# The norm weights travel with x's first tile, and ACT's first transfer is the first key piece

## The chip, the cores and the metric

The kernel runs on one core of one Trainium2 chip. The metric is the device time of one execution in microseconds (us), lower is better. Before the change it is 1268.42 us, the median of three runs (1268.10 to 1268.46).

## The reference, cut to what matters

The reference is a trunk of two layers on x of 512 positions by 1024 features, in float32. Each layer is a token mixer (attention in the first, retention in the second) and a gated MLP. Every one of these four parts begins with an RMS norm that has a weight vector of its own, two vectors for each layer:

```python
def rmsnorm(x, g):
    xf = x.astype(jnp.float32)
    y = xf * lax.rsqrt(jnp.mean(xf * xf, axis=-1, keepdims=True) + EPS)
    return (y * g.astype(jnp.float32)).astype(x.dtype)

for i in range(DEPTH):
    h = rmsnorm(x, norm1_g[i])
    x = x + (attention or retention)(h, ...)
    h = rmsnorm(x, norm2_g[i])
    x = x + conv_ffn(h, ...)
```

What the change touches is the very first step: h = x times norm1_g[0], and the product of h with the key and value columns (256 of them) of attn_w_qkv. The root of the mean square is applied later, to the products.

## The kernel before, in words

x lies transposed in eight tiles of 128 features by 512 positions. Each fp32 operand of a large product is split into two fp32r parts: ACT writes the high part (h_hi, w_hi), DVE the rest (h_lo, w_lo), and `mm3` makes three matmuls of each product (L1293 to L1295). The kernel is one program for each engine, written out in order by hand, with semaphores between them. PE is almost never idle after the first microseconds.

The stage in question is the start. TensorE waits for a zeroed buffer (DVE memset, L677) and then makes WARM_MMS products of zeros, 256 columns wide (L1331); each fp32 product shows in the trace as two passes. It then runs the key and value products: for each of eight feature tiles k, twelve matmuls with 256 columns (four position tiles by three), as soon as w_lo of key piece k (L683) and h_lo of tile k (L662) are there. After these come the query products with 512 columns, in the same way, and so on to the end.

Who brings what in: SP's queue issues, in this order, x tile 0, x tile 1, key piece 2, x tile 2, key piece 3 and so on (L279, L263), and then the first query weights (L282, L283). ACT's queue issues the gain vectors (L337), key piece 0 and key piece 1 (L263), because KV_ACT is 2. An x tile has rows of 2048 bytes, a key piece rows of 1024 bytes, and the gains rows of 128 bytes, always over 128 partitions.

ACT's own order at the start is: its three issues, a small activation that brings its table in (L371), the wait for the gains, then h_hi of tile 0 (L348), w_hi of key piece 0 (L380), w_hi of key piece 1, h_hi of tile 1, and so on. DVE's order is h_lo of tile 0 (L662), w_lo of key piece 0 (L683), w_lo of piece 1, h_lo of tile 1, and so on. Both engines read the gain vectors as a column scalar (`gain[:, norm, m:m + 1]`) in every norm of the kernel, and ACT's wait covers DVE too, since DVE waits for h_hi.

Of the kernel before, what the change touches and what calls it, by code (L numbers as in the profile page):

```python
# [29 lines left out]
P = 128  # L30
D = 1024
S = 512
KT = D // P
# [18 lines left out]
KVC = 256  # L52
KV_ACT = 2
WARM_COLS = 256
WARM_MMS = 6


PAIR_KV = 0
# [21 lines left out]
ROW_F0, ROW_R, ROW_HEAD, ROW_F1 = 0, 1, 2, 1 + R_HEADS  # L80


def trunk(nc, xT, w_kv, w_q, w_ao, w_up0, w_dn0, w_ret, w_up1, w_dn1, gains, conv, gain_col, gain_rot, sinks,
          ident_d, rot_a, rot_r, decay, root_mem, out):
    ctx = ExitStack()
    with ctx:
        def sb(name, shape, dt=F32, scope=ctx):
            return scope.enter_context(nc.sbuf_tensor(name, shape, dt))

        def sem(name):  # L90
            return ctx.enter_context(nc.semaphore(name))


        x = sb("x", [P, KT, S])
        h_hi = sb("h_hi", [P, KT, S], F32R)
        h_lo = sb("h_lo", [P, KT, S], F32R)
        raw = sb("raw", [P, 2, UW])
        w_hi = sb("w_hi", [P, 2, UW], F32R)
        w_lo = sb("w_lo", [P, 2, UW], F32R)
        gain = sb("gain", [P, 4, KT])  # L100
        cvec = sb("cvec", [P, 2, FT, 8])
        ident = sb("ident", [P, P])
        ones = sb("ones", [P, 1])
# [77 lines left out]


        x_in = [sem(f"x_in{k}") for k in range(KT)]
        g_in = sem("g_in")
        c_in = sem("c_in")
        r_in = sem("r_in")
        o_out = sem("o_out")
# [68 lines left out]
        def kv_cols(k):  # L256
            return 1, slice(k * KVC, (k + 1) * KVC)

        def kv_load(eng, k):
            if k < KT:  # L260
                s, cols = kv_cols(k)
                landed = w_loaded[1] if k == KT - 1 else kv_in[k]
                eng.dma_start(raw[:, s, cols], w_kv[:, cols]).then_inc(landed, 16)  # L263
# [8 lines left out]
        @block.sync  # L272
        def _(sp):
            def load(src, pair, s, cols):
                sp.wait_ge(w_lo_ok, 2 * pair + s - 1)
                sp.dma_start(raw[:, s, 0:cols], src).then_inc(w_loaded[s], 16)

            for k in range(KT):
                sp.dma_start(x[:, k, :], xT[k]).then_inc(x_in[k], 16)  # L279
                if k + 1 >= KV_ACT:  # L280
                    kv_load(sp, k + 1)
            sp.dma_start(raw[:, 0, 0:UW // 2], w_q[0][:, 0:UW // 2]).then_inc(q_in, 16)  # L282
            sp.dma_start(raw[:, 0, UW // 2:UW], w_q[0][:, UW // 2:UW]).then_inc(w_loaded[0], 16 * (PAIR_Q + 1))  # L283
            load(w_q[1], PAIR_Q, 1, UW)
            for s in range(2):
                load(w_q[2 + s], PAIR_Q + 1, s, UW)
            for j in range(2):
                for s in range(2):
                    load(w_ao[2 * j + s], PAIR_WO + j, s, UW)

            def rows(src, i):
                return src[bass.ds(i, 1), :, :].rearrange("o p f -> (o p) f")

            def spread(row, which):

                sp.wait_ge(row_ok, row + 1)
                sp.dma_start(root_mem, root[:, :]).then_inc(row_out, 16)
                sp.wait_ge(row_out, 16 * row + 16)
                sp.dma_start(rbc[:, which, :],
                             root_mem.rearrange("t p -> (t p)").unsqueeze(0).to_broadcast([P, S])).then_inc(row_in, 16)  # L300

            def mlp(layer, w_up, w_dn):
                for j in range(2):
                    for s in range(2):
                        load(w_up[2 * j + s], PAIR_UP[layer] + j, s, UW)
                spread(ROW_F1 if layer else ROW_F0, 0)
                with sp.Fori(2, FT // 2) as j:
                    for s in range(2):
                        load(rows(w_up, 2 * j + s), PAIR_UP[layer] + j, s, UW)
                with sp.Fori(0, KT) as j:  # L310
                    for s in range(2):
                        load(rows(w_dn, 2 * j + s), PAIR_DN[layer] + j, s, DW)

            mlp(0, w_up0, w_dn0)
            for j in range(2):
                for s in range(2):
                    load(w_ret[2 * j + s], PAIR_RET + j, s, UW)
            spread(ROW_R, 0)
            for j in range(2, 4):
                for s in range(2):  # L320
                    load(w_ret[2 * j + s], PAIR_RET + j, s, UW)
            with sp.Fori(0, R_HEADS - 1) as h:
                for i in range(4):
                    for s in range(2):
                        load(rows(w_ret, 8 * h + 2 * (4 + i) + s), PAIR_RET + 4 * h + 4 + i, s, UW)
                        if i == 0 and s == 0:
                            spread(ROW_HEAD + h, 1)
            mlp(1, w_up1, w_dn1)
            for m in range(KT):
                sp.wait_ge(xe_ok, XE_DN1 + m + 1)  # L330
                sp.dma_start(out[m], x[:, m, :]).then_inc(o_out, 16)
            sp.wait_ge(o_out, 16 * KT)
# [1 line left out]

        @block.scalar
        def _(act):
            act.dma_start(gain[:, :, :], gains).then_inc(g_in, 16)  # L337
            for k in range(KV_ACT):
                kv_load(act, k)

# [29 lines left out]
            act.wait_ge(warm_ok, 1)  # L370
            nc.scalar.activation(warm[:, :], warm[:, :], ACT.Copy)  # L371

            act.wait_ge(g_in, 16)
            for k in range(KT):
                s, cols = kv_cols(k)
                if k == 0:
# [51 lines left out]
            def exps(g):  # L428
                _, n = GROUPS[g]
                nk = CHUNK if n == 0 else P  # L430
                r = g % 2
                act.wait_ge(dm_ok, g + 1)
                if g >= 2:
                    act.wait_ge(pn_ok, g - 1)
                for i in range(4):
                    c0 = i % 2 * P
                    nc.scalar.activation(ex[:, r, i, 0:nk], ps[:, score_bank(g, i // 2), c0:c0 + nk], ACT.Exp,
                                         scale=A_SCALE, bias=nm[:, r, i:i + 1], accum_out=sm[:, r, i:i + 1])
                nc.scalar.activation(es[:, r, :], dm[:, r, :], ACT.Exp).then_inc(ex_ok, 1)
# [850 lines left out]
        def _(pe):  # L1290
# [38 lines left out]
            pe.wait_ge(zero_ok, 1)  # L1329
            for _ in range(WARM_MMS):  # L1330
                nc.tensor.matmul(ps[:, 6, 0:WARM_COLS], sq[:, 0, 0:P], sq[:, 0, 0:WARM_COLS], start=True, stop=True)  # L1331
# [479 lines left out]
```

## Time and profile before

| | before |
|---|---|
| median of three runs | 1268.42 us |
| the profiled execution's own time | 1268.73 us |
| its span | 1266.5 us |
| what lies around the span | 2.23 us |
| PE busy | 1259.6 us (99%) |
| PE busy from 0 to 8.58 us | 6.75 us |

The span runs from the first to the last instruction of the profiled execution. Times in rows are microseconds from the span's start. PE is TensorE's matmuls, PEld its weight loads, DVE is VectorE, ACT is ScalarE, and a name with a q behind it is the sequencer of that engine, which issues its transfers.

### The profile page before, as it was taken

How to read it: one execution, taken by the hardware profiler on the slowest of the kernel's cores; microseconds unless marked ns; L12 is line 12 of the kernel's file. 1: busy time of each engine (PE TensorE's matmuls, PEld its weight loads, DVE VectorE, ACT ScalarE, POOL GpSimd, SP SyncE). 2: the span in 40 equal slices, each digit the busy share in tenths (PEclk: the TensorE clock that was granted, in tenths of full speed). 3: DMA queues.
4: the chain of work that ended last, by engine and by line, in shares of the span. 5: the costliest groups of instructions: out<-in, count | busy, mean ns of one | idle time of the engine just before them, and what ended most of it. 6: DMA issues, size and time to landing. Idle time of an engine off the chain costs nothing.

```text
span 1266.5 us, 15563 instructions
## 1 busy us (share of the span) xinstructions
PE 1259.6 (99%) x5858; PEld 1041.7 (82%) x5858; DVE 713.5 (56%) x906; ACT 465.4 (37%) x655; POOL 141.8 (11%) x138
## 2 busy tenths in 40 slices
PE   9999999999999999999999999999999999999999
PEld 8777888888888888888888888888888888888887
DVE  6776576677664333545535634634676677663221
ACT  5654454444442223233233223223454444442120
POOL 3651300000000001402102201201000000000000
PEclk9999999999999999999999999999999999999999
DMA  6102232222222323312222222221232222222322
GB/s 244 68 34 69 98 108 99 99 98 86 86 80 96 103 91 135 145 68 100 95 79 75 99 99 75 100 69 65 100 108 99 99 92 88 87 80 96 106 91 89
DMA packets 21909, 120.43 MB, mean 95 GB/s; under 512 B 2680, under 2 KB 3728, under 8 KB 11120
## 3 DMA queue, kind: packets, MB, share of 16 engines
q1 hardware_dynamic: 20928, 117.72, 26.5%
q10 hardware_dynamic: 720, 1.85, 0.4%
q8 instruction: 25, 0.41, 0.1%
q0 software_dynamic: 224, 0.35, 0.1%
q14 instruction: 12, 0.10, 0.0%
HBM read 117.81 MB, written 2.11 MB: 95 GB/s over the span
## 4 chain that ended last, share of the span: by engine, by line
PE 99%; DMA 0%; ACT 0%; DVE 0%; ACTq 0%; issue 0%
PE ps L1293 32%; PE ps L1295 32%; PE ps L1294 32%; PE ps L1413 1%; PE ps L1391 1%; PE ps L1400 1%; PE ps L1310 0%; DMA raw<-in_w_kv 0%; PE ps L1374 0%; PE ps L1364 0%; PE ps L1323 0%; ACT va L404 0%; DVE h_lo L662 0%; DVE x L945 0%; PE ps L1317 0%; ACT h_hi L348 0%
## 5 line engine op out<-in xcount | busy, mean ns | idle before, releaser
L1293 PE MATMUL ps<-h_hi,w_hi 128*128 128x512 f32 x960 | 375.3, 391 | 0.0
L1295 PE MATMUL ps<-h_hi,w_lo 128*128 128x512 f32 x960 | 373.6, 389 | 0.0
L1294 PE MATMUL ps<-h_lo,w_hi 128*128 128x512 f32 x960 | 373.5, 389 | 0.0
L657 DVE TENSOR_TENSOR w_lo<-raw,w_hi 128x2048 fp32r<-128x2048 f32 (+1 forms) x115 | 244.3, 2124 | 141.8 <-ACT w_hi L344 141.8
L344 ACT ACTIVATE w_hi<-raw 128x2048 fp32r<-128x2048 f32 (+1 forms) x115 | 202.6, 1762 | 211.9 <-PE ps L1295 211.9
L1293 PEld LDWEIGHTS ps<-h_hi,w_hi 128*128 128x128 f32 x960 | 180.3, 188 | 37.5
L1295 PEld LDWEIGHTS ps<-h_hi,w_lo 128*128 128x128 f32 x960 | 180.2, 188 | 37.6
L1294 PEld LDWEIGHTS ps<-h_lo,w_hi 128*128 128x128 f32 x960 | 180.3, 188 | 36.6
L1295 PE MATMUL ps<-g_hi,w_lo 128*128 128x512 f32 x352 | 136.9, 389 | 0.0
L1293 PE MATMUL ps<-g_hi,w_hi 128*128 128x512 f32 x352 | 136.9, 389 | 0.0
L1294 PE MATMUL ps<-g_lo,w_hi 128*128 128x512 f32 x352 | 136.9, 389 | 0.0
L532 ACT ACTIVATE y<-u,cvec 128x512 f32<-128x512 f32 x88 | 71.2, 816 | 144.1 <-DVE u L909 76.8
L1293 PE MATMUL ps<-w_hi,h_hi 128*128 128x512 f32 (+1 forms) x224 | 85.7, 383 | 1.0 <-issue 0.8
L1295 PE MATMUL ps<-w_hi,h_lo 128*128 128x512 f32 (+1 forms) x224 | 84.0, 375 | 0.0
L1294 PE MATMUL ps<-w_lo,h_hi 128*128 128x512 f32 (+1 forms) x224 | 83.9, 374 | 0.0
L1295 PEld LDWEIGHTS ps<-g_hi,w_lo 128*128 128x128 f32 x352 | 66.1, 188 | 13.8
L1294 PEld LDWEIGHTS ps<-g_lo,w_hi 128*128 128x128 f32 x352 | 66.1, 188 | 13.7
L1293 PEld LDWEIGHTS ps<-g_hi,w_hi 128*128 128x128 f32 x352 | 66.1, 188 | 13.6
L915 DVE SCALAR_TENSOR_TENSOR y<-u,cvec,y 128x512 f32<-128x512 f32 x88 | 65.5, 748 | 19.8 <-ACT y L532 19.8
L911 DVE TENSOR_TENSOR u<-ps,rbc 128x512 f32<-128x512 f32 x44 | 30.3, 690 | 75.1 <-PE ps L1295 75.1
L539 ACT ACTIVATE g_hi<-gp 128x512 f32 (+1 forms) x44 | 27.8, 632 | 117.5 <-DVE gp L925 117.5
L1142 POOL TENSOR_TENSOR ssum<-sq 128x512 f32<-128x512 f32 x6 | 12.2, 2028 | 479.8 <-ACT sq L561 259.9
(161 smaller groups left out, 1431.7 us busy)
## 6 DMA issues: line engine op xcount, KB each, us to landing
raw<-in_w_up SPq DMA_DIRECT2D x44, 1024.0 KB, 4.8
raw<-in_w_ret SPq DMA_DIRECT2D x32, 1024.0 KB, 4.8
raw<-in_w_dn SPq DMA_DIRECT2D x32, 704.0 KB, 4.0
raw<-in_w_ao SPq DMA_DIRECT2D x4, 1024.0 KB, 4.6
raw<-in_w_q SPq DMA_DIRECT2D x3, 1024.0 KB, 5.3
x<-in_xT SPq DMA_DIRECT2D x8, 256.0 KB, 5.1
out<-x SPq DMA_DIRECT2D x8, 256.0 KB, 5.0
rbc<-root_mem SPq DMA_DIRECT2D x6, 256.0 KB, 3.1
```

Of the source, the lines that this page charges most:

```text
L344: nc.scalar.activation(w_hi[:, s, 0:cols], raw[:, s, 0:cols], ACT.Copy).then_inc(w_hi_ok, 1)
L532: nc.scalar.activation(y[:, ab, :], u[:, ab, 2:S + 2], ACT.Identity, scale=c[:, 0:1], bias=c[:, 1:2]).then_inc(yb_ok, 1)
L539: nc.scalar.activation(g_hi[:, bass.ds(i, 1), :].rearrange("p o f -> p (o f)"), gp[:, :], ACT.Copy).then_inc(ghi_ok, 1)
L657: nc.vector.tensor_tensor(w_lo[:, s, 0:cols], raw[:, s, 0:cols], w_hi[:, s, 0:cols].bitcast(F32), ALU.subtract).then_inc(w_lo_ok, 1)
L911: nc.vector.tensor_tensor(u[:, 1, 2:S + 2], ps[:, 2 * s + 1, :], rbc[:, 0, :], ALU.mult).then_inc(u_ok, 1)
L915: nc.vector.scalar_tensor_tensor(y[:, ab, :], u[:, ab, 1:S + 1], c[:, 4 * ab + 1:4 * ab + 2], y[:, ab, :], ALU.mult, ALU.add).then_inc(y1_ ...
L1293: nc.tensor.matmul(dst, st[0], mv[0], start=start, stop=False)
L1294: nc.tensor.matmul(dst, st[0], mv[1], start=False, stop=False)
L1295: return nc.tensor.matmul(dst, st[1], mv[0], start=False, stop=stop)
L1391: last = nc.tensor.matmul(ps[:, score_bank(g, par), i * P:i * P + nk], qT[rows, n, j:j + 2, :].rearrange("p j q -> p (j q)"), keys[rows, c ...
L1400: last = nc.tensor.transpose(ps[:, TT_BANK, i * P:(i + 1) * P], pn[:, g % 2, i, :], ident[:, :])
L1413: last = nc.tensor.matmul(ps[par * A_DH:(par + 1) * A_DH, PV_BANK, 0:4 * CHUNK], v[:, n // 2, c * A_DH:(c + 1) * A_DH], pT[:, g % 2, par * ...
```

## The change

The gain vectors get no transfer, no semaphore and no tensor of their own. One SBUF tensor `gain_x` has 32 columns of gains (128 bytes for each partition) in front of x's eight tiles; `gain` and `x` are now views of it. In HBM the gains stand in front of each row of x's first tile, so SP's first transfer has rows of 2176 bytes and brings both. ACT's queue begins with key piece 0. The zero products are five in place of six. Everything else, the order on each engine among it, stays.

```diff
-WARM_MMS = 6
+WARM_MMS = 5
+GAINS = 4 * KT
...
-        x = sb("x", [P, KT, S])
+        gain_x = sb("gain_x", [P, GAINS + KT * S])
+        gain = gain_x[:, 0:GAINS].rearrange("p (n k) -> p n k", k=KT)
+        x = gain_x[:, GAINS:GAINS + KT * S].rearrange("p (k s) -> p k s", s=S)
...
-        gain = sb("gain", [P, 4, KT])
...
-        g_in = sem("g_in")
...
             for k in range(KT):
-                sp.dma_start(x[:, k, :], xT[k]).then_inc(x_in[k], 16)
+                if k == 0:
+                    sp.dma_start(gain_x[:, 0:GAINS + S], x_first).then_inc(x_in[k], 16)
+                else:
+                    sp.dma_start(x[:, k, :], xT[k - 1]).then_inc(x_in[k], 16)
...
         def _(act):
-            act.dma_start(gain[:, :, :], gains).then_inc(g_in, 16)
             for k in range(KV_ACT):
                 kv_load(act, k)
...
-            act.wait_ge(g_in, 16)
...
-    arrays["xT"] = c(A(x)[0].T.reshape(KT, P, S))
+    x_tiles = A(x)[0].T.reshape(KT, P, S)
+    gains = np.stack([A(norm1_g)[0], A(norm2_g)[0], A(norm1_g)[1], A(norm2_g)[1]])
+    gains = gains.reshape(4, KT, P).transpose(2, 0, 1).reshape(P, GAINS)
+    arrays["x_first"] = c(np.concatenate([gains, x_tiles[0]], 1))
+    arrays["xT"] = c(x_tiles[1:])
```

## Rows read from the trace of the kernel before

**Rows 1.** The page, busy time, share of the span and instructions of each engine.

```profile
PE 1259.6 (99%) x5858; PEld 1041.7 (82%) x5858; DVE 713.5 (56%) x906; ACT 465.4 (37%) x655; POOL 141.8 (11%) x138
```

**Rows 2.** PE's waits: who waited for whom, us in total, times, longest.

```profile
PE ps L1364 <- ACT va L404: 1.5, 1, 1.5
...
PE ps L1293 <- issue: 0.8, 1, 0.8
```

**Rows 3.** PE by stages: window, its length, busy (instructions), granted clock, DMA share, GB/s.

```profile
8.58:24.35 15.77, 15.77 (x111) 1.00 0.78 285
```

**Rows 4.** The chain that ended last, in order: start us, us, what.

```profile
0.75 0.42 ACTq L337
1.20 0.45 ACTq L263
1.68 4.91 DMA raw<-in_w_kv
6.61 0.42 ACT w_hi L380
...
7.68 0.76 DVE h_lo L662
...
8.58 0.36 PE ps L1293
...
33.45 0.60 ACT sqq L413
```

**Rows 5.** Timeline, 0 to 14 us: start, us, engine, line, operation [idle before it, releaser].

```profile
3.70 0.72 ACT L348 ACTIVATE h_hi<-x,gain 128x512 fp32r<-128x512 f32 x1
...
4.46 0.75 DVE L662 SCALAR_TENSOR_TENSOR h_lo<-x,gain,h_hi 128x512 fp32r<-128x512 f32 x1 [3.27 <-ACT h_hi L348]
...
5.77 0.42 ACT L380 ACTIVATE w_hi<-raw 128x256 fp32r<-128x256 f32 x1 [1.35 <-DMA raw<-in_w_kv]
...
6.22 0.43 DVE L683 TENSOR_TENSOR w_lo<-raw,w_hi 128x256 fp32r<-128x256 f32 x1 [1.01 <-ACT w_hi L380]
...
6.75 0.36 PE L1293 MATMUL ps<-w_hi,h_hi 128*128 128x256 f32 x1 [0.84 <-issue]
...
8.13 0.28 PE L1295 MATMUL ps<-w_hi,h_lo 128*128 128x256 f32 x1
```

**Rows 6.** Transfers issued from 0 to 1, at 1.2, at 2.15: KB, us to landing.

```profile
x<-in_xT SPq DMA_DIRECT2D x1, 256.0 KB, 2.7
gain<-in_gains ACTq DMA_DIRECT2D x1, 16.0 KB, 2.9
...
x<-in_xT SPq DMA_DIRECT2D x1, 256.0 KB, 4.4
raw<-in_w_kv ACTq DMA_DIRECT2D x1, 128.0 KB, 4.5
...
x<-in_xT SPq DMA_DIRECT2D x1, 256.0 KB, 4.9
```

**Rows 7.** DMA queues, 2.0 to 3.2, then 3.2 to 4.6: packets, MB, share of engines.

```profile
q1 hardware_dynamic: 162, 0.30, 73.9%
q10 hardware_dynamic: 155, 0.03, 12.1%
...
q10 hardware_dynamic: 175, 0.16, 35.2%
```

**Rows 8.** Zero products' weight loads by stages: window, length, busy (loads), clock, DMA, GB/s.

```profile
1.82:3.53 1.71, 1.33 (x4) 1.00 0.87 283
...
5.09:5.30 0.21, 0.19 (x1) 1.00 0.88 195
```

**Rows 9.** Timelines of ACT, DVE and PE, 12.4 to 26 us.

```profile
13.58 1.06 ACT L386 ACTIVATE w_hi<-raw 128x1024 fp32r<-128x1024 f32 x1 [0.41 <-DMA raw<-in_w_q]
...
17.83 4.67 DVE L700 TENSOR_TENSOR ssum<-ssum,qn 128x512 f32<-128x512 f32 x6
...
24.19 0.95 PE L1310 MATMUL ps<-ones,ssum 128*128 128x1 f32 x8
```

More of the change, by code:

```diff
@@ L80, with trunk @@
 ROW_F0, ROW_R, ROW_HEAD, ROW_F1 = 0, 1, 2, 1 + R_HEADS
-def trunk(nc, xT, w_kv, w_q, w_ao, w_up0, w_dn0, w_ret, w_up1, w_dn1, gains, conv, gain_col, gain_rot, sinks,
+def trunk(nc, x_first, xT, w_kv, w_q, w_ao, w_up0, w_dn0, w_ret, w_up1, w_dn1, conv, gain_col, gain_rot, sinks,
           ident_d, rot_a, rot_r, decay, root_mem, out):
@@ L1781 @@
     arrays["w_ret"] = c(np.concatenate(units))
-    arrays["gains"] = c(np.stack([A(norm1_g)[0], A(norm2_g)[0], A(norm1_g)[1], A(norm2_g)[1]])
-                        .reshape(4, KT, P).transpose(2, 0, 1))
     cw = np.concatenate([A(ffn_conv_w)[:, :, 0, :], A(ffn_conv_b)[:, None, :]], 1)
@@ L1804 @@
     by = dict(zip(names, args))
-    trunk(nc, by["xT"], by["w_kv"], by["w_q"], by["w_ao"], by["w_up0"], by["w_dn0"], by["w_ret"], by["w_up1"],
-          by["w_dn1"], by["gains"], by["conv"], by["gain_col"], by["gain_rot"], by["sinks"], by["ident"],
+    trunk(nc, by["x_first"], by["xT"], by["w_kv"], by["w_q"], by["w_ao"], by["w_up0"], by["w_dn0"], by["w_ret"], by["w_up1"],
+          by["w_dn1"], by["conv"], by["gain_col"], by["gain_rot"], by["sinks"], by["ident"],
           by["rot_a"], by["rot_r"], by["decay"], root_mem, out)
```

## The prediction

> **What bounds the kernel now.** I read the engines' shares on the page first: PE is busy for 99% of the span [rows 1]. Then the waits of PE alone, because with such a share only the places where PE stands idle can give time back. There are few: 1.5 us for ACT's copies of the values, 0.8 us ahead of the first real matmul, and what is left lies at the start [rows 2]. The view by stages shows that from 8.58 us PE works without a gap, 15.77 of 15.77 us [rows 3]. So the kernel's end moves with the instant at which this unbroken run begins, as long as what comes later moves along or has room.
>
> The chain of waits says what sets that instant, 8.58 us [rows 4]. ACT's queue spends 0.42 us on the gains, issues key piece 0 at 1.20 and key piece 1 at 1.68. Piece 1 lands 4.91 us later, near 6.6; ACT makes its high part at 6.61, DVE ends h_lo of tile 1 after 7.68 + 0.76, and PE's second group starts at 8.58. That is 1.97 us from piece 1's landing to PE. The timeline shows the group ahead of it: ACT idles 1.35 us until key piece 0 is in at 5.77, w_lo follows at 6.22 and PE at 6.75; the group's last matmul starts at 8.13 [rows 5]. Eleven steps in 1.38 us are 0.125 us for a matmul, so the group takes 12 x 0.125 = 1.50 us, PE is free at 8.25, and it waits 0.33 us for tile 1.
>
> **The change, part by part.**
>
> The gains' issue goes. ACT's two key pieces are issued 0.45 us sooner (1.20 - 0.75), at 0.75 and 1.20 [rows 4]. If each transfer still took 4.5 and 4.9 us to land [rows 4, 6], that would be all, 0.45 us.
>
> The gains' rows leave ACT's queue (q10), and they weigh more than their bytes. From 2.0 to 3.2 us q10 moved 155 packets with 0.03 MB while SP's q1 moved 162 with 0.30 MB [rows 7]: about one packet of q10 for each of q1, and hardly a key row among them. A packet of q10 took 0.121 x 16 x 1.2 / 155 = 15 ns, one of q1 0.739 x 16 x 1.2 / 162 = 88 ns. So the 128 small rows went out at the pace of x's large ones, and key piece 0, issued 0.45 us behind them, did not start until about 3.2 us, where q10's packets become large (175 with 0.16 MB, 0.352 x 16 x 1.4 / 175 = 45 ns each) [rows 7]. Without the gains key piece 0 starts where they did, near 2.0.
>
> Where do the two pieces land? Piece 0 takes the gains' place, which landed at 0.75 + 2.9 = 3.65 [rows 6]. It shares each of the 16 DMA engines with x tile 0, eight packets of each: they cost 8 x (45 - 15) = 0.24 us more than the gains' did, and x's rows are 6% longer, 8 x 88 x 0.0625 = 0.04 us. Both land about 0.3 us later: x tile 0 at 0.75 + 2.7 + 0.3 = 3.75, piece 0 at 3.95. Piece 1 takes the place that piece 0 has now. That one started at 3.2 beside x tile 1 and landed at 1.20 + 4.5 = 5.7 [rows 6]. Piece 1 can start when piece 0's rows are through, some 0.1 to 0.3 us later at most than piece 0 does now; I take 5.8, against 6.6 now.
>
> The first group. ACT's h_hi of tile 0 starts at 3.80 in place of 3.70, hidden now by nothing but the early landing. DVE's h_lo follows 0.76 later, 4.56, and takes 0.75; w_hi of piece 0 is made in that time, and w_lo can start at about 5.3. PE begins 0.53 us after w_lo's start, as now (6.22 to 6.75) [rows 5]: 5.8 instead of 6.75. It ends its group at 5.8 + 1.50 = 7.3.
>
> The second group. Piece 1's high part at 5.8 plus the 1.97 us of the chain gives 7.8. This is later than 7.3, so it decides: PE's unbroken run begins at 7.8, 0.8 us sooner. The ends for this term: 0.45 us from the issue alone, and 1.3 us (8.58 - 7.3) if the second group is never late. I take 0.8, because piece 0's own row of before shows what a piece takes that starts at that place in q10. x tile 1 landed at 1.20 + 4.4 = 5.6 [rows 6] and is wanted just after piece 1.
>
> One zero product less. It has two passes. The weight loads come four in 1.71 us at first, 0.43 us apart, and one in 0.21 us from 5.09 [rows 8]. The granted clock stands at 1.00, 2.4 GHz, in both rows, but the spacing halves, so I read the low level (1.2 GHz) up to about 4.9. Six products occupy PE until 5.73 (three passes from 5.09), five until about 5.3. Neither is in the way of a start at 5.8: costed at nothing, covered by the wait for w_lo. If PE could start before 5.7 the sixth would cost up to 0.43 us. The other bound is a lost clock, the last rival below.
>
> The longer first transfer costs x tile 0 its 0.04 us, counted above; the freed wait on the gains' semaphore costs and saves nothing, since h_hi now waits for the same landing. The 128 bytes by which x's tiles shift in SBUF show no counterpart in any row: I cost them at 0, within 0.1 us either way.
>
> Is anything late next? x tile 2, issued by 2.15, lands at 7.05 [rows 6]; 0.76 + 0.76 us of h_hi and h_lo later it is 8.6, and PE comes for it at 7.8 + 1.50 = 9.3. The first query weights do not move: ACT gets them at 13.58, and behind them DVE works to 17.83 + 4.67 = 22.50 on the sum of squares, which PE takes at 24.19 [rows 9]. That cover shrinks from 1.7 to 0.9 us and holds. The wait at 33.45 is ACT's square of a bank that PE has just finished [rows 2, 4], so it moves with PE. The 0.8 us then reach the end.
>
> The Trainium skill, DMA: Bandwidth & Descriptors, section "Issuing engines are not separate DMA queues", says that transfers from SP and ACT interleave on the same 16 DMA engines, and that issuing from several engines saves no more than the sequencer's time. By that rule taken strictly the gain is the issue's 0.45 us. The trace agrees with the interleaving, and it shows that small rows hold up those behind them in their queue, which the rule leaves out.
>
> **The sum.** 1268.73 - 0.8 = 1267.9 us for a profiled execution. The median of the runs is 0.31 us below the profiled one, so the forecast for it is 1268.42 - 0.8 = 1267.6 us. A measurement of this kernel tells about 0.2% from no change, which is 2.5 us (1265.9 to 1271.0); all of the above lies within it.
>
> **The rivals.**
>
> Only the issue counts. The landing of a transfer is its issue plus 4.5 to 4.9 us for all of these pieces [rows 4, 6], as if by a common delay. For it: the four numbers from 4.4 to 4.9 lie close together. Against it: x tile 0 and the gains took 2.7 and 2.9, so it is the load ahead that makes the rest. Time 1268.42 - 0.45 = 1268.0.
>
> Hidden anyway. A slow DMA engine, not the queue's order, makes the last packets late: x tile 1 and piece 0 land at 5.6 and 5.7 though they share no queue. If piece 1's last packet stays with that engine's backlog, it lands at 6.5 as now. For it: a landing is that of the last of 16. Against it: fewer packets are then ahead of it. Time 1268.4.
>
> Slower, by the clock. The spacing of the passes halves near 4.9, in the last third of the zero products [rows 8]. With five, PE's work ends at 5.3 and it idles to 5.8. If the rise comes later in an execution than here, and this idle stretch withholds it, the key products run at 1.2 GHz: 0.25 us each in place of 0.125, 1.5 us more for a group of twelve. The first slow group ends at 5.8 + 3.0 = 8.8, against 8.58 for the second group's start now, so one slow group already eats the gain (+0.2); the point from which it decides is a second one. Two give 11.8 against 8.58 + 1.5 = 10.1, 1.7 us slower, 1270.1; three give 3.2 us slower, 1271.6, beyond the bound. Against it: the rise shown comes ahead of the tenth pass, which stays, and the idle stretch gets shorter, 0.5 us in place of about 1.0. TensorE: Matmul & The Clock Gate of the Trainium skill, Part 1, says that the moment of the rise varies by about half a microsecond from run to run, since the monitor runs free of the kernel's start; no run here shows that so far.
>
> **How the numbers follow.** The forecast (0.6 to 1.3 us saved) 0.60, only the issue 0.20, hidden anyway 0.13, the clock 0.07. The range: 1.3 us saved and 0.2 for the scatter of runs give 1266.9 at the low end; "hidden anyway" with that scatter gives 1268.6 at the high end. About one in ten is left out, the clock and a little at the low end. Only three slow groups would be slower by over 0.2%, 0.04 with what I do not see; faster by over 0.2% would want 2.5 us, more than the start holds, 0.02; within 0.2% 0.94.
>
> **What would show each step.** The first large activation of ACT (L380) at 4.4 to 4.6 and no longer idle for 1.35 us; the second near 5.8; PE's first real matmul at 5.8 and the first of the unbroken run at 7.8; no small packets in q10; the two pieces landing about 3.2 and 4.6 us after issue; the zero products' last passes still 0.21 us apart; the 1.5 us wait for the values unchanged. It is wrong if piece 1 lands after 6.2, if key products show 0.25 us spacing, or if PE waits between 9 and 33 us.

## The result, and the profile after

The change makes the kernel slower: 1278.43 us against 1268.38 us (medians of six runs each), ratio 1.0078 with a 95% interval from 1.0068 to 1.0088. That is 10.05 us, and the profiled span grew by 9.8 us, from 1266.5 to 1276.3. I had forecast 0.8 us less, in a range from 1266.9 to 1268.6.

I first looked at the start, where all my steps were. These are PE's waits after the change, in us: total, times, longest.

```profile
PE ps L1366 <- ACT va L406: 1.5, 1, 1.5
PE ps L1333 <- DVE sq L679: 1.2, 1, 1.2
PE ps L1295 <- DVE w_lo L685: 0.4, 1, 0.4
```

And this is the timeline of the changed kernel's start, where the rows answer to [rows 5].

```profile
4.30 0.72 ACT L351 ACTIVATE h_hi<-gain_x 128x512 fp32r<-128x512 f32 x1 [1.12 <-DMA gain_x<-in_x_first]
...
5.05 0.75 DVE L664 SCALAR_TENSOR_TENSOR h_lo<-gain_x,h_hi 128x512 fp32r<-128x512 f32 x1 [3.88 <-ACT h_hi L351]
...
5.58 0.42 ACT L382 ACTIVATE w_hi<-raw 128x256 fp32r<-128x256 f32 x1 [0.25 <-DMA raw<-in_w_kv]
...
6.24 0.55 PE L1295 MATMUL ps<-w_hi,h_hi 128*128 128x256 f32 x1 [0.38 <-DVE w_lo L685]
...
7.94 0.28 PE L1295 MATMUL ps<-w_hi,h_hi 128*128 128x256 f32 x1
```

The second group begins at 7.94 us in place of 8.58, and PE no longer waits for it: the start has become 0.64 us shorter. In the first 8.58 us PE was busy for 6.33 us before (the 6.75 of the table of before is that of the first 9.00 us) and for 6.97 after. So some 10.5 us must be lost in the stretch where PE never idles. A stretch without waits can only get longer if its instructions do. The page's groups show it: busy us, behind the comma the mean of one matmul in ns, and behind the second bar the engine's idle us. The operands stand in the order moving, stationary: in `g_hi,w_lo` the columns of g_hi stream past the weights w_lo. The groups of before:

```profile
L1293 PE MATMUL ps<-h_hi,w_hi 128*128 128x512 f32 x960 | 375.3, 391 | 0.0
...
L1295 PE MATMUL ps<-g_hi,w_lo 128*128 128x512 f32 x352 | 136.9, 389 | 0.0
L1293 PE MATMUL ps<-g_hi,w_hi 128*128 128x512 f32 x352 | 136.9, 389 | 0.0
L1294 PE MATMUL ps<-g_lo,w_hi 128*128 128x512 f32 x352 | 136.9, 389 | 0.0
...
L1293 PEld LDWEIGHTS ps<-g_hi,w_hi 128*128 128x128 f32 x352 | 66.1, 188 | 13.6
```

And those of the changed kernel:

```profile
L1295 PE MATMUL ps<-h_hi,w_hi 128*128 128x512 f32 x960 | 375.2, 391 | 0.0
...
L1297 PE MATMUL ps<-g_hi,w_lo 128*128 128x512 f32 x352 | 139.0, 395 | 0.0
L1295 PE MATMUL ps<-g_hi,w_hi 128*128 128x512 f32 x352 | 139.0, 395 | 0.0
L1296 PE MATMUL ps<-g_lo,w_hi 128*128 128x512 f32 x352 | 139.0, 395 | 0.0
...
L1295 PEld LDWEIGHTS ps<-g_hi,w_hi 128*128 128x128 f32 x352 | 66.1, 188 | 16.1
```

The three g groups went from 389 to 395 ns, and their weight loads take what they took but idle 2.2 to 2.5 us more. The h groups have not moved. (A mean runs from a matmul's start to its end, and each overlaps the next: they start about 0.23 us apart in both kernels. What adds up to the kernel's time is the distance from start to start.) Each group of products of o and of a with w went from 49.8 to 50.5 us and from 25.0 to 25.3. So 3 x (352 + 128 + 64) = 1632 matmuls became some 6 ns longer each, and the others did not. What sets these apart: their moving operand (g, o, a) lies behind the place where `gain` was, and their weights ahead of it. The addresses that the program gives them, in bytes of a partition:

```
                 before    after     e1        e2        e3        e6
h_hi             32896     33024     33024     33024     16512     16512
w_hi             82048     82176     82176     82176     65664     65664
g_hi            127872    127872    127872    128000    127872    127936
g_hi - w_hi      45824     45696     45696     45824     62208     62272
  modulo 256         0       128       128         0         0        64
h_hi - w_hi, mod 256   0       0         0         0         0         0
```

The distances of a and o from w, and of the low parts, are the same modulo 256 as that of g_hi. The tensors from x to w_lo moved up by 128 bytes, since the gains now lie ahead of x; `gain` behind w_lo is gone, so everything from cvec on stayed. That is theory A below. Theory B blames the new transfers, theory C the weights' own address.

### The profile page after: what moved, and what is told of

Same layout as the page of the kernel before. It is cut to its first block, busy times and chain, and to the rows that moved or that the text cites. A ratio compares the mean times of both kernels' runs of the same rounds, so it can differ in the third digit from the quotient of the medians.

```text
span 1276.3 us, 15557 instructions
## 1 busy us (share of the span) xinstructions
PE 1270.1 (100%) x5856; PEld 1041.4 (82%) x5856; DVE 713.6 (56%) x906; ACT 465.4 (36%) x655; POOL 141.9 (11%) x138
## 4 chain that ended last, share of the span: by engine, by line
PE 99%; DMA 0%; ACT 0%; DVE 0%; issue 0%
PE ps L1295 32%; PE ps L1297 32%; PE ps L1296 32%; PE ps L1415 1%; PE ps L1393 1%; PE ps L1402 1%; PE ps L1312 0%; PE ps L1376 0%; DMA gain_x<-in_x_first 0%; PE ps L1366 0%; PE ps L1325 0%; ACT va L406 0%; DVE h_lo L664 0%; ACT h_hi L351 0%; DVE gain_x L947 0%; PE ps L1319 0%
## 5 line engine op out<-in xcount | busy, mean ns | idle before, releaser
L1297 PE MATMUL ps<-h_hi,w_lo 128*128 128x512 f32 x960 | 373.6, 389 | 0.0
L1296 PE MATMUL ps<-h_lo,w_hi 128*128 128x512 f32 x960 | 373.5, 389 | 0.0
L1297 PEld LDWEIGHTS ps<-h_hi,w_lo 128*128 128x128 f32 x960 | 180.2, 188 | 37.5
L1296 PEld LDWEIGHTS ps<-h_lo,w_hi 128*128 128x128 f32 x960 | 180.3, 188 | 36.7
L1297 PE MATMUL ps<-g_hi,w_lo 128*128 128x512 f32 x352 | 139.0, 395 | 0.0
L1296 PE MATMUL ps<-g_lo,w_hi 128*128 128x512 f32 x352 | 139.0, 395 | 0.0
L1297 PE MATMUL ps<-w_hi,h_lo 128*128 128x512 f32 (+1 forms) x224 | 84.0, 375 | 0.0
L1296 PE MATMUL ps<-w_lo,h_hi 128*128 128x512 f32 (+1 forms) x224 | 83.9, 375 | 0.0
L1296 PEld LDWEIGHTS ps<-g_lo,w_hi 128*128 128x128 f32 x352 | 66.1, 188 | 16.0
L1297 PEld LDWEIGHTS ps<-g_hi,w_lo 128*128 128x128 f32 x352 | 66.1, 188 | 16.0
```

What stands on the lines that cost most here:

```text
L1296: nc.tensor.matmul(dst, st[0], mv[1], start=False, stop=False)
L1297: return nc.tensor.matmul(dst, st[1], mv[0], start=False, stop=stop)
```

## The experiments

**e1: the layout alone, in the kernel before.**

```diff
+        gain = sb("gain", [P, 4, KT])
         x = sb("x", [P, KT, S])
...
         w_lo = sb("w_lo", [P, 2, UW], F32R)
-        gain = sb("gain", [P, 4, KT])
```

> The kernel before with one edit: the gain tensor is declared ahead of x and no longer behind w_lo. Transfers, waits and zero products stay. h, raw and w move up by 128 bytes in each partition, everything from cvec on stays where it was. Theory A (the distance between the stationary and the moving operand of a matmul, in the products of a, g and o with w, costs time at an odd multiple of 128 bytes): those 1632 matmuls take about 6 ns more each, 9.8 us, so 1278.2 us, with the mean of the g group at 395 ns and of the h group at 389 to 391. Theory B (the new transfers at the start, or what they set off later, cost the time): 1268.4, g group 389 ns. Theory C (the weights' own address counts, not the distance): 1278.2 as well.

Measured: 1278.99 us against 1268.51, ratio 1.0083 (1.0066 to 1.0100). The loss is here without any part of the change but the order of two declarations. Theory B falls. The groups of e1:

```profile
L1293 PE MATMUL ps<-h_hi,w_hi 128*128 128x512 f32 x960 | 375.3, 391 | 0.0
...
L1295 PE MATMUL ps<-g_hi,w_lo 128*128 128x512 f32 x352 | 139.1, 395 | 0.0
```

Its start is that of before, so it gives the price by itself: 1278.99 - 1268.51 = 10.5 us over 1632 matmuls, 6.4 ns each.

**e2: the change, with the old distance restored.**

```diff
         w_lo = sb("w_lo", [P, 2, UW], F32R)
+        pad = sb("pad", [P, 32])
```

> The changed kernel with one edit: an unused tensor of 128 bytes behind w_lo, so that a, g and o stand at the old distance from w while w keeps its new address. Theory A: g group back at 389 ns, and what is left is the start's gain, 0.6 to 0.8 us: 1267.7. Theory B: 1278.4, g group 395 ns. Theory C: 1278.4, g group 395 ns.

Measured: 1267.84 us, ratio 0.9995 (0.9986 to 1.0005), and the weights have the same address as in the slow kernel. That rejects theory C; 128 bytes that nothing uses give back 10.6 us of 1278.43. The group of e2:

```profile
L1298 PE MATMUL ps<-g_hi,w_lo 128*128 128x512 f32 x352 | 136.9, 389 | 0.0
```

**e3: the change, with gain_x behind w_lo.**

```diff
-        gain_x = sb("gain_x", [P, GAINS + KT * S])
-        ...
         w_lo = sb("w_lo", [P, 2, UW], F32R)
+        gain_x = sb("gain_x", [P, GAINS + KT * S])
+        ...
```

> The changed kernel with one edit: gain_x is declared behind w_lo in place of ahead of h_hi, so that h, raw and w lie 16384 bytes lower than before and only x is off by 128 bytes against the others. Theories A and C: 1267.7, g group 389 ns. Theory B: 1278.4. If x's own place (read by ACT and DVE only) counted, something between.

Measured: 1267.84 us, ratio 0.9994 (0.9984 to 1.0004), g group 389 ns. Where x stands, which only ACT and DVE read, costs nothing that shows.

**e4: which distances are slow.** TensorE by itself, with nothing else running, in a single execution of 96 matmuls for each distance. The kernel has no diff; its core is

```python
for m in moving:              # 16 tiles, at 0, 32, ... 896 behind a line
    for i in range(96):
        c = i % 16 * P
        nc.tensor.matmul(ps[:, i % 2, :], w_s[:, c:c + P], m[:, :], start=True, stop=True)
```

> Not the trunk: it computes nothing of the reference and gives x back. TensorE alone makes 96 matmuls of 128x512 fp32r in a row for each of 16 moving tiles that lie at 0, 32, 64, ... 896 bytes behind a line of 1024, first with 16 weight pieces on such a line, then with 16 pieces 128 bytes behind one. Theory A: with the first weights the moving tiles at 128, 384, 640 and 896 take about 6 ns more each, with the second weights those at 0, 256, 512 and 768. Theory C: all tiles alike within one set of weights, the two sets 6 ns apart. Rival to both: no difference anywhere, because it takes the traffic of ACT and DVE as well; then the distance only shows in the trunk.

The groups of e4 (m_h lies 256 bytes past w's line, m_i 320, m_b 64, m_d 128, m_a 32; w_t is 128 bytes past it):

```profile
L69 PE MATMUL ps<-m_a,w_s 128*128 128x512 f32 x96 | 22.6, 395 | 0.0
...
L69 PE MATMUL ps<-m_d,w_s 128*128 128x512 f32 x96 | 22.6, 395 | 0.0
L69 PE MATMUL ps<-m_h,w_t 128*128 128x512 f32 x96 | 22.6, 395 | 0.0
...
L69 PE MATMUL ps<-m_i,w_s 128*128 128x512 f32 x96 | 22.2, 391 | 0.0
...
L69 PE MATMUL ps<-m_b,w_s 128*128 128x512 f32 x96 | 22.1, 391 | 0.0
...
L69 PE MATMUL ps<-m_h,w_s 128*128 128x512 f32 x96 | 21.9, 389 | 0.0
L69 PE MATMUL ps<-m_d,w_t 128*128 128x512 f32 x96 | 21.9, 389 | 0.0
```

m_h is fast with w_s and slow with w_t, m_d the other way round: it is the distance and not the address of either, and no traffic of other engines is needed. I had expected slow times only at odd multiples of 128. In fact a multiple of 256 is the fast case (389 ns), 64 past one is nearly as good (391), and 32, 96, 128, 160, 192 and 224 past one all cost 394 to 396.

**e6: 64 bytes off, in the trunk.**

```diff
         x = gain_x[:, GAINS:GAINS + KT * S]...
+        pad = sb("pad", [P, 16])
         cvec = sb("cvec", [P, 2, FT, 8])
```

> The kernel of e3 with 64 unused bytes behind gain_x, so that a, g and o stand 64 bytes past a multiple of 256 from w. The sweep gave 389 ns at multiples of 256 bytes, 391 at 64 past one and 395 at all other steps of 32. Theory A, in the form that the distance modulo 256 sets the time in the trunk too: 2 to 3 ns more on 1632 matmuls, 3.4 to 5.1 us, so 1271.2 to 1272.9, g group 391 ns. Rival (only whether it is a multiple of 128 or 256 bytes counts, 64 is like 128): 1277.6, 395 ns. Rival (only the odd multiple of 128 is bad in the trunk): 1267.8.

Measured: 1272.53 us, ratio 1.0034 (1.0020 to 1.0047), 4.7 us above e3 and 4.3 above the kernel before beside it (1268.26), inside what theory A said and outside both rivals. It is not 2 ns on all, though:

```profile
L1296 PE MATMUL ps<-g_hi,w_hi 128*128 128x512 f32 x352 | 138.9, 395 | 0.0
L1298 PE MATMUL ps<-g_hi,w_lo 128*128 128x512 f32 x352 | 138.1, 392 | 0.0
L1297 PE MATMUL ps<-g_lo,w_hi 128*128 128x512 f32 x352 | 136.8, 389 | 0.0
```

The three matmuls of a product, in the order L1296, L1297, L1298, stand at 395, 389 and 392, though all three have 64 past a multiple of 256 between their operands. Their average, 392, is near the 391 of the sweep. Why they differ stays open, so the distance modulo 256 is not the whole rule.

**e8: exact distances, near and far.** One weight piece (a second one for nine of the distances, the negative ones among them), 45 groups of 96 matmuls (not 46) in a single execution, the first distance twice; each group has a line of its own, for example

```python
for i in range(REPS):
    last = nc.tensor.matmul(ps[:, i % 2, 0:512], w_low, mv(131072, 512), start=True, stop=True)
```

> Not the trunk: it computes nothing of the reference and gives x back. 96 matmuls in a row with one and the same weight piece for each of 46 exact distances of the moving operand from it: multiples of 256 bytes up to 131072, odd ones from 4 to 320 past 512, negative ones, and 256 and 128 columns. Theory A (modulo 256): 389 ns at all multiples of 256 near and far, of either sign, 391 at 64 past one, 395 else; with fewer columns the same few ns or, where the weight load sets the pace, none. Rival (a larger period, say a bank of several KB): the multiples of 256 differ among themselves, and some distance is faster than 389, which the trunk could use.

Rows of e8: L78 is 131072 bytes, L58 is 768, L124 is -16384, L112 is 0 (weights read from the moving tile itself), L108 is 240 past 512, L94 is 128 past, L80 is 4 past; L132 to L136 have 256 columns, at 0, 64 and 128 past.

```profile
L80 PE MATMUL ps<-big 128*128 128x512 f32 x96 | 22.9, 399 | 0.0
...
L94 PE MATMUL ps<-big 128*128 128x512 f32 x96 | 22.5, 395 | 0.0
...
L112 PE MATMUL ps<-big 128*128 128x512 f32 x96 | 21.9, 389 | 0.0
...
L108 PE MATMUL ps<-big 128*128 128x512 f32 x96 | 21.9, 388 | 0.0
...
L124 PE MATMUL ps<-big 128*128 128x512 f32 x96 | 21.9, 389 | 0.0
L58 PE MATMUL ps<-big 128*128 128x512 f32 x96 | 21.9, 389 | 0.0
...
L78 PE MATMUL ps<-big 128*128 128x512 f32 x96 | 21.9, 389 | 0.0
L132 PE MATMUL ps<-big 128*128 128x256 f32 x96 | 11.7, 283 | 0.0
L136 PE MATMUL ps<-big 128*128 128x256 f32 x96 | 11.6, 281 | 0.0
```

All multiples of 256 are alike, near or far and of either sign, so there is no larger period and no distance clearly faster than the kernel has had. A distance off the 32-byte grid, 240 past, was fast too (388), which the rule "a multiple of 256" does not cover; 16, 80 and 176 past stood at 393 to 394, and 4 past was the slowest (399). With 256 columns the means are 279 to 283 ns in no order of distance, and with 128 columns 274 to 275: there the distance costs nothing that shows.

**e7: the same for sq and ident.**

```diff
+        pad_sq = sb("pad_sq", [P, 16])
         sq = sb("sq", [P, 2, S])
...
+        pad_rbc = sb("pad_rbc", [P, 48])
         rbc = sb("rbc", [P, 2, S])
```

> The kernel of e3 with sq moved by 64 bytes and all from rbc on by 256, so that sq too stands at a multiple of 256 bytes from ident (it stood 192 past one); all other distances keep their class. A version meant to beat both kernels. Theory A: the 64 transposes with sq as an operand take up to 6 ns less each, 0.4 us at most: 1267.4 to 1267.8. Rival: with 128 columns the weight load sets the pace, no change, 1267.8.

Measured: 1268.31 us, ratio 1.0000 (0.9991 to 1.0009); the 64 transposes take 281 ns as in e3. That is what the rival said, in line with the 128 columns of e8. The time is 0.5 us above the rival's 1267.8, and 0.3 above e5, which was measured beside it; this edit moved more tensors than sq, and what costs the 0.3 us stays open.

**e5 and e9: the zero products.** e5 is e3 with `WARM_MMS = 6`, e9 the kernel before with `WARM_MMS = 5`.

> The kernel of e3 (the change with gain_x behind w_lo) with six zero products again. If the sixth product only fills a wait, as the prediction's step says: the same 1267.8 us within 0.2, PE's first real matmul at 6.2 as in e3. Rival: the sixth makes PE late, because at the low clock it takes 0.85 us and ends near 6.1 to 6.3: up to 0.3 us slower. Other rival: five leave the clock's rise later and cost the first group time, six are then up to 0.5 us faster, and in the profile the first real matmuls are 0.12 us apart and not 0.21.

> The kernel before with five zero products in place of six, nothing else. The prediction's step (the wait for w_lo covers either number): no change, 1268.4 within 0.3, PE's first real matmul between 6.0 and 6.8 as before. Rival (the clock's rise is lost with five): the first groups at 0.21 to 0.25 us a matmul and up to 1.7 us slower. Its transfers are those of before, so its profile is one more sample of when key pieces 0 and 1 are in: near 5.0 to 5.8 and 6.6 to 7.0.

Measured: e5 1267.99 us, ratio 0.9998 (0.9989 to 1.0007); e9 1268.31 us, ratio 1.0001 (0.9991 to 1.0010). Neither number of products shows in the time. In e5's profile the passes of zeros were still 0.43 us apart up to about 6 us and end only near 6.7, and the first real matmul starts at 6.38, 0.2 us later than in e3 (6.17), as the first rival said; its second group is no later for it (7.97 against 8.12). In e9's the first real matmul starts at 5.79, earlier than I had said, because key piece 0 was in by 4.8 us.

**e10, e11, e12: the start by itself.** e10 is the kernel before with the gains issued last on ACT's queue:

```diff
-            act.dma_start(gain[:, :, :], gains).then_inc(g_in, 16)
             for k in range(KV_ACT):
                 kv_load(act, k)
+            act.dma_start(gain[:, :, :], gains).then_inc(g_in, 16)
```

e11 is e3 once more, e12 the kernel before once more, both without an edit.

> The kernel before with the gains issued behind the two key pieces on ACT's queue. Theory (the gains' 128 small rows go out one for one with x's rows and hold up the pieces behind them): the pieces land as in the changed kernel, 3.6 to 3.8 and 4.0 to 4.4 us after their issue, and the gains only near 5.3. Rival (only the 0.45 us of the issue counts): 4.5 and 4.9 us after their issue. ACT's first tile now waits for the gains, so PE starts no earlier than 6.8 and the time is 1268.4 to 1269.2 either way.

> The kernel of e3 once more, beside e9 on one chip, for the size of the start's gain by itself: unbroken run of PE from 7.7 to 8.0 in place of 8.6 to 9.0, so 0.5 to 0.8 us faster than before, 1267.6 to 1268.0; in executions where the clock rises after 6.3 only 0.1 to 0.4 of it is left.

> The kernel before, unchanged, one look: how far the landings of the key pieces and the clock's rise scatter between two executions of the same program. Key piece 0 in at 5.0 to 5.8, piece 1 at 6.6 to 7.0, the zero products' passes 0.43 us apart up to somewhere between 4.6 and 6.5.

Measured: e11 1267.89 us, ratio 0.9996 (0.9987 to 1.0005). e12 ran once, 1269.27 us. e10 ran once, 1271.21 us, 2 us above my bound. The chain of e12:

```profile
1.68 5.50 DMA raw<-in_w_kv
7.21 0.42 ACT w_hi L380
...
9.17 0.36 PE ps L1293
```

Piece 1 is in at 7.2 us here, later than the 6.6 to 7.0 that I had said, against 6.6, 6.7 and 7.0 in the three other profiles with the old transfers (before, e9, e1), and at 5.4 to 6.0 in those with the new ones. Piece 0 landed 4.5 us after its issue in before, but 3.8, 3.8 and 3.6 in e1, e12 and e9, and 3.6 to 3.8 with the new transfers. e10's landings:

```profile
x<-in_xT SPq DMA_DIRECT2D x1, 256.0 KB, 3.6
raw<-in_w_kv ACTq DMA_DIRECT2D x1, 128.0 KB, 3.8
```

Its piece 1 took 4.5 us, where the four profiles with the gains ahead have 4.9 to 5.5 and those with the new transfers 4.2 to 4.7. Its gains came in at 6.2 us and not near 5.3, so PE had to wait until 8.17. All its transfers began to move late: from 1.8 to 2.1 us the DMA share was 0.00, against 0.66 in before, so up to 0.3 us of each of its landings is not due to the order.

And the stages of e10 (window, length, PE busy, granted clock, DMA, GB/s):

```profile
6.00:8.00 2.00, 0.29 (x2) 1.00 1.06 391
8.00:9.00 1.00, 0.83 (x7) 1.00 1.06 391
9.00:10.00 1.00, 1.00 (x8) 0.57 1.08 382
10.00:11.00 1.00, 1.00 (x7) 0.50 1.07 372
11.00:12.00 1.00, 1.00 (x6) 0.50 1.08 418
12.00:13.00 1.00, 1.00 (x9) 0.73 1.02 406
```

PE had nothing to do from about 6.3 to 8.17 us. Its key products then started 0.12 us apart until 9.1, and after that the granted clock fell to 0.50 of full speed, 1.2 GHz, and they stood 0.21 us apart for about 3.5 us. The unbroken run began 0.41 us sooner than in before and the span is still 2.5 us longer (1269.0 against 1266.5), so this cost about 2.9 us, an estimate from these two spans. It is a relative of the prediction's third rival and not the same: there an idle stretch withholds the clock's rise, here the clock had risen and was lost again. In e1 and e12 PE idled for 1.3 us before its second group and the granted clock stayed at 1.00.

## Why the prediction was wrong, point by point

**The step that failed** is the last sentence on the longer transfer: "The 128 bytes by which x's tiles shift in SBUF show no counterpart in any row: I cost them at 0, within 0.1 us either way." The shift was 128 bytes, but not of x alone: h, raw, w_hi and w_lo moved with it and a, g and o did not. Its price is 10.5 us (e1). I bounded an effect by its absence from the rows of one layout, which can't show it, and did not ask which distances between operands the edit changes. A list of addresses before and after would have put the question; no row of before could have answered it. The signs of being wrong that I had listed all lay in the start or in PE's waits, and a longer matmul shows in neither.

**What bounds the kernel** was read rightly, and it is why the loss comes through in full: PE is busy for 99% of the span, so 6.4 ns on each of 1632 matmuls go to the end undiminished. I used the unbroken run only for its beginning; its pace was the larger lever.

**The start's gain** held in sign and nearly in size: 0.64 us in the profile for the 0.8 forecast, 7.94 for 7.8. That 7.94 is near 7.8 is partly luck. I had the second group start when tile 1 is ready, with PE waiting for it from 7.3. In the changed kernel the first group started at 6.24 and not at 5.8, its first steps were slow, and it ended at 7.94; DVE had h_lo of tile 1 done at 7.39 (6.64 + 0.75). So the second group went by the first one's end, and piece 1 no longer decided it. Over the profiles, the spans with the new transfers and the old distance are 1265.7, 1266.0, 1265.8, 1266.5 and 1265.7 (e2, e3, e5, e7, e11), mean 1265.9; with the old transfers 1266.5, 1266.6 and 1267.1 (before, e9, e12), mean 1266.7. In the timed runs it is 0.67 (e2, e3), 0.37 (e11), 0.27 (e5) and -0.05 us (e7), and every one of the intervals includes no gain at all.

**Its parts** came out otherwise. Piece 1 came in at 5.58 where I had 5.8. Piece 0 needed 3.7 us where I had 3.2. The row that I built on, 4.5 us, was one draw: three further executions with the gains ahead of it have 3.6 to 3.8, so for piece 0 the rival "only the issue counts" is the better account, and my reading that the gains' small rows held it up is not borne out. Piece 1 gained more than the issue, about 1.2 us (6.9 on average to 5.7); e10, with 4.5 us from its issue, points to the gains' rows for the rest, in one execution. x tile 0 became dearer than I said, 3.5 us for 3.0, and its landing now heads PE's chain. I had put the sharing with key piece 0 at 0.24 us. In e10, with its rows unchanged but key piece 0 beside it, it took 3.6; less the late start of up to 0.3 us, that leaves at least 0.6 of the 0.9 us over before (2.7) to the sharing. So that term was too small; the price of the longer rows by themselves was not measured.

**The zero products** cost and save nothing, as costed (e5, e9). The clock rival did not cause the loss, but a late rise does happen: e3's first key products stood 0.21 us apart (start us, us, what),

```profile
6.72 0.21 PE ps L1296
6.94 0.21 PE ps L1297
7.15 0.19 PE ps L1295
7.34 0.12 PE ps L1296
```

against 0.12 us from there on. The granted clock stands at 1.00 in that stretch too, so the rise is read from the spacing, as in the prediction: after 7.1 us in e3, near 6.6 in the changed kernel, near 4.9 in before, near 4.6 in e2. The Trainium skill, TensorE: Matmul & The Clock Gate, Part 1, gives the scatter of the rise as about half a microsecond to either side; over these profiles it spans 2.5 us.

**A page's rule that the runs contradict.** The same page of the Trainium skill, TensorE: Matmul & The Clock Gate, says in Part 2, "Step-by-step: what each phase is for", that the array has two independent SBUF read ports and that loading the next weights takes no read bandwidth from the running matmul. Were that all, the distance between the two could not matter. e4 and e8 have only these two reads going on, and the distance costs 6 to 10 ns of some 230 from one matmul's start to the next (22.5 to 22.9 us for 96 in place of 21.9). So the two reads do affect each other; in which part of the hardware, no run here shows.

## What to carry to other kernels

When an edit adds, removes or moves a tensor, list the SBUF addresses before and after, and look at the distance between the stationary and the moving operand of every large fp32r product: keep it a multiple of 256 bytes (tried here for fp32r alone). In a kernel that TensorE bounds, compare the mean of one matmul by operand before looking for waits; 6 ns in 395 is easy to miss and was 0.8% of the time. A landing time from a single profile is one draw, here with 0.5 to 0.9 us of scatter, and can't carry a term of that size.

## What the runs showed of the hardware that I had not expected

- A run of 128x512 fp32r matmuls takes 21.9 us for 96 when the moving operand lies a multiple of 256 bytes from the weights, and 22.5 to 22.9 at most other distances; at 64 past a multiple 22.1 to 22.2, at 16, 80 and 176 past 22.3 to 22.4, and at 240 past 21.9. The multiples of 256 are alike from -16384 to 131072 bytes, and with 256 or 128 columns no effect shows (e4, e8).
- The granted clock fell to 0.50 after PE had been idle for most of 6.3 to 8.2 us (e10), and the time was 1271.21 us in that execution.
- The change with 128 unused bytes behind w_lo, or with gain_x behind it, is the version to keep: 1267.84 us in both, 10.6 us better than the change as it was made. Against the kernel before (1268.51 beside them) it is 0.7 us less, which these runs can't tell from no difference.
